# Moving the start addresses of a float32r kernel's tiles in SBUF: weights at 160 and 192, rows at 448 or 192, modulo 512

## The chip, the cores and the metric

One core of one Trainium2 chip. The metric is the device time of one execution in microseconds (us), as the median of several runs. A page of the profile and its trace come from one execution taken by the hardware profiler.

## The reference: what is computed

Two blocks, one after the other, on 256 latent tokens and 256 context tokens of width 1024. Almost all arithmetic is in dense products with weights that are read once from HBM:

```
# first block: layer 0 a gated linear attention (gla), layer 1 a state-space scan (ssd)
for i in range(2):
    m = split(silu(c) @ ada_w[i] + ada_b[i], 6)
    u = modulate(h, m[0], m[1])
    y = gla_mixer(u, ...) if i == 0 else ssd_mixer(u, ...)      # h @ w_in, a scan, @ w_out
    h = layer_norm(ALPHA * h + m[2] * y)
    h = layer_norm(ALPHA * h + m[5] * (relu(modulate(h) @ ffn_w1[i]) ** 2 @ ffn_w2[i]))
# second block: two attention layers, three kinds of attention each
for l in range(2):
    hn = rms_norm(h) * (1 + scale) + shift
    q, k, v, z, gm = split(hn @ w_in[l])          # neighbourhood, latent (mla), differential
    y = sum(sigmoid(gm[r]) * ((attend_r * silu(z[r])) @ w_br[l][r]) for r in range(3))
    h = h + gate * (y @ w_out[l])
```

## The kernel before, in words

**One product.** A float32 product is made of three float32r matmuls, which are called passes here. The weights are split into a rounded part `weights_hi` and the rest `weights_lo`, and the rows (the activations) into two tiles of the same kind: `input_hi` and `input_lo`, or `ffn_hidden_hi` and `_lo`, `ssd_out_hi` and `_lo`, `mix_o_hi` and `_lo`, `merge_o_hi` and `_lo`. For each block of 128 features the method `passes` lists

```
out += [(hi[:, k, cols], xh), (hi[:, k, cols], xl), (lo[:, k, cols], xh)]
```

where the first of a pair is the stationary operand (128 columns, loaded by a LDWEIGHTS) and the second is the moving one (512 columns for all tokens, 256 where only the latent ones are left). The value projections are made by token instead (`passes_by_token`): there the rows are stationary and the weights move, 512 columns of them. Eight blocks of 128 features make 24 passes, which fill one bank of PSUM. Line 284 (`product`) issues most passes; lines 305, 322, 3586 and 3736 issue the others. While a pass runs, the LDWEIGHTS of the next one is under way.

**The weights' way.** SP's queue loads 512 KB at a time into one of four slots of `wslots`. ScalarE (ACT) copies a slot into `weights_hi`, rounding it (line 221). VectorE (DVE) or GpSimd (POOL) subtracts and writes `weights_lo` (line 231). TensorE (PE) waits for the split, and a slot comes free when it is split. An order written out by hand sets what each engine does; nothing plans it at run time.

**The stages.** The times are those of the profiled execution. GLA input products and scan (about 35 to 300 us), its output product (300 to 350), the feed-forward of layer 0 over all tokens (350 to 720), the SSD layer (720 to 1110), the feed-forward of layer 1 over latent tokens (1110 to 1300), attention layer 0 over all tokens (1300 to 1950), attention layer 1, in its latter part over latent tokens (1950 to 2455).

**Addresses.** Every tile is taken with `b.sb(stack, name, shape)`, one behind the other, as a stack in each partition; each starts at a multiple of 32 bytes. 16,512 bytes lie in front of `wslots`, so that it starts at 128 modulo 512. All large tiles are multiples of 512 bytes, so the start modulo 512 is handed on from tile to tile until a small one moves it. Counted from the shapes, the starts modulo 512 before are:

| tiles | stage | start modulo 512 |
|---|---|---|
| wslots, weights_hi, weights_lo | all | 128 |
| input_hi, input_lo | GLA input | 0 |
| gla_out_hi, gla_out_lo | GLA output | 0, 96 |
| input_hi, input_lo, ffn_hidden_hi, _lo | feed-forward of layer 0 | 448 |
| input_hi, input_lo, ssd_out_hi, _lo | SSD | 320 |
| input_hi, input_lo, ffn_hidden_hi, _lo, mix_o_hi, _lo, merge_o_hi, _lo | feed-forward of layer 1 and both attention layers | 320 |

The operand of one pass or another lies a multiple of 512 bytes behind its tile's start. For a pair of tiles this document calls the moving tile's start minus the stationary tile's start, modulo 256, its offset; the prediction says why 256 is used.

Of the kernel before, what the change touches and what calls it, by code (L numbers as in the profile page):

```python
# [14 lines left out]
F32 = mybir.dt.float32  # L15
# [5 lines left out]
P = 128  # L21
# [9 lines left out]
DEPTH = 2  # L31
# [8 lines left out]
SH = SG * SREP  # L40
# [5 lines left out]
NAH, MLH, DFH = 8, 8, 4  # L46
# [14 lines left out]
AM = 2 * SLOT // P  # L61
SHARED = {"halves_ready": "unit_scaled", "rank_rounded": "hat_edges", "norm_summed": "tables_made", "roped": "hat_factors", "mixed_gated": "maps_combined", "mixed_squared": "rows_final", "power_added": "rows_ready", "vectors_added": "unit_made", "group_summed": "unit_scaled", "group_turned": "top_made", "group_flat": "top_ready",
          "group_copied": "prob_ready", "group_biased": "prob_scaled", "group_shifted": "prob_turned",
          "sum_slab_0": "maps_combined", "sum_slab_1": "rows_final", "sum_slab_2": "rows_ready", "sum_slab_3": "rows_turned"}
ADA_ROUND = {"ada_front": 0, "ada_core": 1, "ada_scan": 3}


# [306 lines left out]
def build(nc, d, out, dump=None, until=99):  # L374
    ctx = ExitStack()
    with ctx:
        b = Build(nc, d, ctx)
        b.psum = ctx.enter_context(nc.psum_tensor("psum", [P, 8, 512], F32))
        b.wslots = b.sb(ctx, "wslots", [P, RAW, SLOT])
        b.whi = b.sb(ctx, "weights_hi", [P, RING, SLOT])  # L380
        b.wlo = b.sb(ctx, "weights_lo", [P, RING, SLOT])
        b.whi_r, b.wlo_r = b.whi[:].bitcast(F32R), b.wlo[:].bitcast(F32R)
        b.H1 = b.sb(ctx, "h1", [P, KD, T])
        b.H2 = b.sb(ctx, "h2", [P, KD, T])
        b.ident = b.sb(ctx, "ident", [P, P])
        b.snake = b.sb(ctx, "snake", [P, P])
        b.ones = b.sb(ctx, "ones", [P, P])
        b.half_ones = b.sb(ctx, "half_ones", [P, P])
        b.cols = b.sb(ctx, "cols", [P, 5, P])
        b.eps = b.sb(ctx, "eps", [P, 2])  # L390
        b.mod1 = b.sb(ctx, "mod1", [P, DEPTH, 48, 2])
        b.mod2 = b.sb(ctx, "mod2", [P, DEPTH, 24, 2])
        b.lam = b.sb(ctx, "lam", [P, DEPTH, 4])
        make_plan(b)
        with ExitStack() as early:
            b.ada_c = b.sb(early, "ada_c", [P, 2, KD, 32])
            b.ada_flat = b.sb(early, "ada_flat", [P, 512])
            b.ada_vec = b.sb(early, "ada_vec", [P, AM, 2])
            with b.joined():
                gla_layer(b)  # L400
                if until >= 3:
                    finish_layer(b, 0, ALL, None)
                if until >= 4:
                    ssd_layer(b)
        with ExitStack() as late:
            input_parts(b, late, False)
            if until >= 5:
                finish_layer(b, 1, LAT, b.H2)
            if until >= 6:
                with b.joined():  # L410
                    for l in range(DEPTH):
                        attention_layer(b, l, out)
        if until < 6:
            store_stage(b, b.H2 if until >= 5 else b.H1, out, dump)
# [122 lines left out]
def ada_copy(b, act, phase, r, bank):  # L537

    g = b.phases[phase][2] + r
    before = ADA_ROUND[phase] + r  # L540
    act.wait_ge(b.sem("product_done"), g + 1)
# [315 lines left out]
def input_parts(b, st, raw=None):  # L857

    b.UH = b.sb(st, "input_hi", [P, KD, T])
    b.UL = b.sb(st, "input_lo", [P, KD, T])  # L860
    b.UH_r, b.UL_r = b.UH[:].bitcast(F32R), b.UL[:].bitcast(F32R)
    if raw is not False:
        b.raw = b.sb(st, "input_raw", [P, 2, T]) if raw is None else raw
# [534 lines left out]
def gla_layer(b):  # L1398
    st = ExitStack()
    with st:  # L1400
        qk = b.sb(st, "gla_qk", [P, GH, 2, T])
        v = b.sb(st, "gla_v", [P, TT, D])
        gate = b.sb(st, "gla_gate", [P, KD, T])
        cum = b.sb(st, "gla_cum", [P, 2, GH, T])
        qT, kT = qk[:, :, 0, :], qk[:, :, 1, :]
        stat = b.sb(st, "gla_stat", [P, GH, TT])
        oT = qk[:].rearrange("p h a t -> p (h a) t")
        room = [x[:].rearrange(s) for x, s in ((qk, "p h a t -> p (h a t)"), (v, "p t n -> p (t n)"),
                                               (gate, "p k t -> p (k t)"), (cum, "p z h t -> p (z h t)"))]
        gla_project(b, qT, kT, v, gate, cum, room)  # L1410
        at = b.nc.sbuf_base
        b.UH, b.UL = (b.nc.alloc_sbuf_tensor_at(f"gla_out_{x}", [P, KD, T], F32, offset=at + o) for x, o in (("hi", 4096), ("lo", OUT_LOW)))
        b.UH_r, b.UL_r = b.UH[:].bitcast(F32R), b.UL[:].bitcast(F32R)
        gla_core(b, qk, v, cum, oT, stat)
        gla_out(b, oT, gate, stat)
# [200 lines left out]
def gla_core(b, qk, v, cum, oT, stat):  # L1616
# [12 lines left out]
    st = ExitStack()  # L1629
    with st:  # L1630
# [12 lines left out]
        masks = b.sb(st, "gla_masks", [P, NR, P], U8)  # L1643
        diag2 = b.sb(st, "gla_diag2", [P, P])
        middles = b.sb(st, "gla_middles", [P, 2, 2, GH, CH])
        vec = b.ada_vec[:].rearrange("p (q t) v -> p q t v", q=4)
        wide_masks = b.H2[:, 0:3, :].rearrange("p a t -> p (a t)").rearrange("p (z n k) -> p z n k", z=2, k=P)
        _, _, vt, _ = b.phases["gla_v1"]
        OUT, STATE, SCORE, TURNED, ADA = (0, 1), (2, 3), (4, 5), 6, 7
# [481 lines left out]
def ssd_layer(b):  # L2131
    st = ExitStack()
    with st:
        xs = b.sb(st, "ssd_x", [P, TT, SDI])
        bt = b.sb(st, "ssd_b", [P, NCTX // P, SG * SN])
        bT, cT = b.H2[:, :, NCTX:T], b.H1[:, :, 0:NCTX]
        z = b.sb(st, "ssd_z", [P, SDI // P, NLAT])
        y = xs[:, 0:2, :]
        s = b.sb(st, "ssd_state", [P, 2, SDI])
        tok = b.sb(st, "ssd_tok", [P, 6, 2 * SH])  # L2140
        dskip = b.sb(st, "ssd_dskip", [P, SH])
        rows = b.sb(st, "ssd_rows", [P, 3 * P])
        pick = b.sb(st, "ssd_pick", [P, 2 * SH])
        unit = b.sb(st, "ssd_unit", [P, P])
        hide = b.sb(st, "ssd_hide", [P, 2, P])
        ssd_project(b, xs, bt, bT, cT, z, s, tok, dskip, rows, pick, unit, hide)
        power = b.sb(st, "ssd_power", [P, 2, NLAT])
        ssd_core(b, xs, bt, bT, cT, y, z, s, tok, dskip, rows, pick, unit, hide, power)
        ssd_out(b, y, s, power)
# [192 lines left out]
def ssd_core(b, xs, bt, bT, cT, y, gates, s, tok, dskip, rows, pick, unit, hide, power):  # L2342
# [16 lines left out]
    st = ExitStack()  # L2359
    with st:  # L2360
# [1 line left out]
        square = b.H2[:, 0:4, 0:NCTX].rearrange("p (i n) t -> p i n t", i=2)  # L2362
        work = mixers[:, 0:4 * SDI].rearrange("p (a n) -> p a n", a=4)
        part = b.H2[:, :, 0:NCTX]
        vec = b.ada_vec[:].rearrange("p (q t) v -> p q t v", q=4)
        SEGS, SCORE, ADA = 3, 4, 3

        def main(g):
# [937 lines left out]
def attend_pairs(b, l, r, m, last, fill):  # L3306
# [6 lines left out]
    groups = [(seg, t) for seg in ((LAT,) if last else (LAT, CTX)) for t in range(2)]  # L3313
# [4 lines left out]
    early = 0 if near else S // 3 if last else S // 2  # L3318
# [3 lines left out]
    st = ExitStack()  # L3322
    with st:
        prob = b.sb(st, "prob", [P, 2, 2, T])
        probT = m["spare"] if r else b.sb(st, "probT", [P, 2, T])
        top = b.sb(st, "row_top", [P, 2, 2, 2])
        den = b.sb(st, "row_sum", [P, 2, 2])
        if near:
            bias, biased = b.H1[:, 0:2, :], b.H1[:, 2:4, :]
            mask = b.sb(st, "na_mask", [P, NLAT])  # L3330
# [460 lines left out]
def attend_maps(b, l, m, last, fill):  # L3791
# [3 lines left out]
    groups = [(s, t) for s in ((LAT,) if last else (LAT, CTX)) for t in range(2)]  # L3795
# [3 lines left out]
    early, lead = S // 2, min(S + S // 2, 2 * KD)  # L3799
# [19 lines left out]
    st = ExitStack()  # L3819
    with st:  # L3820
        prob = b.sb(st, "prob", [P, 2, 2, T])
        probT = b.sb(st, "probT", [P, T])
        top = b.sb(st, "row_top", [P, 2, 2, 2])
        den = b.sb(st, "row_sum", [P, 2, 2])
        sub = b.sb(st, "diff_rows", [P, DFH, P])
        ss = b.sb(st, "diff_ss", [P, len(groups), DFH])
        sq = b.sb(st, "diff_sq", [P, DFH, P])
        with b.stage() as block:

# [464 lines left out]
```

## Time and profile before

| | |
|---|---|
| median of three runs | 2463.5 us (2460.54 to 2468.15) |
| the profiled execution, its own time | 2456.91 us |
| its span in the trace | 2455.1 us |
| PE busy | 2355.8 us, 96% of the span, 13,654 matmuls |
| PEld (weight loads) busy | 1932.6 us, 79% |
| DVE busy | 1570.2 us, 64% |
| ACT busy | 1217.1 us, 50% |
| POOL busy | 450.7 us, 18% |
| granted TensorE clock, mean | 0.985 |
| DMA | 302 MB, 123 GB/s |

A matmul's busy time in the trace is its own duration with the end modelled; neighbours overlap. How fast PE goes through passes is therefore read from their starts: the time from one start to the next is called the pitch here.

### The profile page before, as it was taken

The page shows a single profiled execution, that of the slowest core. Times are in us where ns is not written, and L with a number is a line of the kernel's source. Part 1 is how long each engine was busy: PE and PEld are TensorE (multiplying, and loading weights), DVE is VectorE, ACT ScalarE, POOL GpSimd, SP SyncE. Part 2 cuts the span into 40 slices and gives each one's busy share as a digit, 9 for nine tenths or more (in the row PEclk, how much of TensorE's full clock was granted, in tenths as well). Part 3 has the DMA queues.
Part 4 walks back from the last instruction along what each step waited for, and adds up shares of the span by engine and source line. Part 5 has one row for each costly group of instructions (what it writes and reads, how often), then busy time and mean ns, then how long its engine had stood idle before and what let it go on. Part 6 is the DMA issues. An engine that isn't in the chain of part 4 may idle for free. (4 is left out here: it accounts for less than half of the span.)

```text
span 2455.1 us, 34875 instructions
## 1 busy us (share of the span) xinstructions
PE 2355.8 (96%) x13654; PEld 1932.6 (79%) x13654; DVE 1570.2 (64%) x2359; ACT 1217.1 (50%) x2090; POOL 450.7 (18%) x277
## 2 busy tenths in 40 slices
PE   7998999999999999989999999999999989989989
PEld 5776778887879888689998767677777877878778
DVE  5867978778765667687665454643665455574665
ACT  2666544223238334557454355763365244665464
POOL 0000000000017434000004431005111145404210
PEclk9999999999999999999999999999999999999999
DMA  8734527666535332446663232213222234334334
GB/s 316 212 121 145 156 80 212 184 185 186 158 102 138 95 92 62 138 138 195 185 179 86 77 85 59 64 50 94 74 64 77 77 97 116 95 89 118 94 96 129
DMA packets 416075, 302.11 MB, mean 123 GB/s; under 512 B 10210, under 2 KB 389192, under 8 KB 414888
## 3 DMA queue, kind: packets, MB, share of 16 engines
q1 hardware_dynamic: 414800, 299.45, 42.0%
q8 instruction: 109, 1.79, 0.3%
q10 hardware_dynamic: 1112, 0.44, 0.1%
q14 instruction: 54, 0.44, 0.1%
HBM read 298.80 MB, written 1.05 MB: 122 GB/s over the span
## 5 line engine op out<-in xcount | busy, mean ns | idle before, releaser
L221 ACT ACTIVATE weights_hi<-wslots 128x1024 fp32r<-128x1024 f32 (+1 forms) x408 | 427.1, 1051 | 251.4 <-PE psum L284 192.2
L284 PE MATMUL psum<-input_hi,weights_hi 128*128 128x512 f32 (+1 forms) x1384 | 494.9, 358 | 1.6 <-PEq L1044 0.6
L284 PE MATMUL psum<-input_hi,weights_lo 128*128 128x512 f32 (+1 forms) x1384 | 482.8, 349 | 0.0
L284 PE MATMUL psum<-input_lo,weights_hi 128*128 128x512 f32 (+1 forms) x1384 | 482.1, 348 | 0.0
L231 POOL TENSOR_TENSOR weights_lo<-wslots,weights_hi 128x1024 fp32r<-128x1024 f32 (+1 forms) x139 | 333.6, 2407 | 714.5 <-ACT weights_hi L221 713.8
L231 DVE TENSOR_TENSOR weights_lo<-wslots,weights_hi 128x1024 fp32r<-128x1024 f32 x269 | 330.3, 1237 | 161.1 <-ACT weights_hi L221 160.3
L284 PEld LDWEIGHTS psum<-input_hi,weights_hi 128*128 128x128 f32 x1384 | 261.8, 189 | 45.5 <-issue 8.8
L284 PEld LDWEIGHTS psum<-input_lo,weights_hi 128*128 128x128 f32 x1384 | 261.2, 189 | 38.1 <-issue 2.9
L284 PEld LDWEIGHTS psum<-input_hi,weights_lo 128*128 128x128 f32 x1384 | 261.0, 189 | 37.0
L284 PE MATMUL psum<-ffn_hidden_hi,weights_hi 128*128 128x512 f32 (+1 forms) x512 | 173.6, 339 | 0.0
L284 PE MATMUL psum<-ffn_hidden_hi,weights_lo 128*128 128x512 f32 (+1 forms) x512 | 172.5, 337 | 0.0
L284 PE MATMUL psum<-ffn_hidden_lo,weights_hi 128*128 128x512 f32 (+1 forms) x512 | 171.7, 335 | 0.0
L2849 DVE RECIPROCAL head_rstd<-head_rstd 128x512 f32<-128x512 f32 (+1 forms) x32 | 94.4, 2951 | 96.0 <-ACT head_rstd L2841 96.0
L3736 PE MATMUL psum<-input_hi,weights_hi 128*128 128x512 f32 (+1 forms) x384 | 135.9, 354 | 4.4 <-issue 3.3
L3736 PE MATMUL psum<-input_lo,weights_hi 128*128 128x512 f32 (+1 forms) x384 | 130.9, 341 | 0.0
L3736 PE MATMUL psum<-input_hi,weights_lo 128*128 128x512 f32 (+1 forms) x384 | 130.8, 340 | 0.0
L284 PEld LDWEIGHTS psum<-ffn_hidden_hi,weights_hi 128*128 128x128 f32 x512 | 96.8, 189 | 13.3 <-issue 3.6
L284 PEld LDWEIGHTS psum<-ffn_hidden_hi,weights_lo 128*128 128x128 f32 x512 | 96.5, 189 | 10.7
L284 PEld LDWEIGHTS psum<-ffn_hidden_lo,weights_hi 128*128 128x128 f32 x512 | 96.1, 188 | 10.8 <-issue 0.2
L1306 ACT ACTIVATE ffn_hidden<-psum 128x512 f32<-128x512 f32 (+1 forms) x64 | 31.4, 490 | 124.5 <-PE psum L284 117.1
L2323 DVE SCALAR_TENSOR_TENSOR ssd_conv<-psum,cols,ssd_conv 128x508 f32<-128x508 f32 (+3 forms) x128 | 87.2, 681 | 4.5
L3736 PEld LDWEIGHTS psum<-input_hi,weights_hi 128*128 128x128 f32 x384 | 73.8, 192 | 17.1 <-issue 7.8
(541 smaller groups left out, 4915.9 us busy)
## 6 DMA issues: line engine op xcount, KB each, us to landing
wslots<-w_in SPq DMA_DIRECT2D x132, 512.0 KB, 3.9
wslots<-ffn_w SPq DMA_DIRECT2D x128, 512.0 KB, 4.6
wslots<-ssd_w_in SPq DMA_DIRECT2D x49, 512.0 KB, 4.0
wslots<-ada_w SPq DMA_DIRECT2D x32, 512.0 KB, 4.7
h<-w_ada SPq DMA_DIRECT2D x28, 512.0 KB, 4.3
wslots<-gla_w_in SPq DMA_DIRECT2D x25, 512.0 KB, 4.8
input_raw<-ada_w SPq DMA_DIRECT2D x24, 512.0 KB, 4.0
ada_slab<-ada_w SPq DMA_DIRECT2D x24, 512.0 KB, 3.8
```

Of the source, the lines that this page charges most:

```text
L221: act.activation(self.part(self.whi_r, n), self.slot(n), ACT.Copy)\
L231: engine.tensor_tensor(self.part(self.wlo_r, n), self.slot(n), self.part(self.whi, n), ALU.subtract)\
L284: ins = pe.matmul(out_of(self.bank(g)), l, r, start=first and i == 0, stop=last and i == len(pairs) - 1, skip_group_check=not (first and l ...
L1306: act.activation(hid[:, j % NH, :], b.bank(g)[:, a:e], ACT.Relu).then_inc(b.reads_out(g), 1)
L2323: ins = dve.scalar_tensor_tensor(dst[:, :, o], src[:, :, i], tap(k), dst[:, :, o], ALU.mult, ALU.add)
L2849: dve.reciprocal(r, r).then_inc(b.tick("dve_step"), 1)
L3736: ins = pe.matmul(b.bank(g)[:, a:e], w, u, start=x == 0, stop=x == len(pairs) - 1, skip_group_check=True)
```

## The change

Only the places of tiles in SBUF change. `lam` (32 bytes) is taken ahead of `weights_hi`, and `eps` (8 bytes, which take 32) ahead of `weights_lo`. The small tile `ada_vec` of the early layers, and the tiles `row_top`, `row_sum` and `diff_ss` of the attention stages, become views of one tile `small` (128 bytes) that stays for the whole program. `ssd_dskip` goes to the very top of SBUF. The starts modulo 512 after it are:

| tiles | before | after |
|---|---|---|
| wslots | 128 | 128 |
| weights_hi | 128 | 160 |
| weights_lo | 128 | 192 |
| input_hi, input_lo of GLA | 0 | 0 |
| gla_out_hi, gla_out_lo | 0, 96 | 0, 96 |
| rows of the feed-forward of layer 0 | 448 | 448 |
| rows of SSD | 320 | 192 |
| rows of the feed-forward of layer 1 and of attention | 320 | 448 |
| h1, h2, ident, ones | 128 | 192 |

No instruction is added, removed or moved: on all five engines the same instructions stand in the same order with the same waits, and the names of the small tiles alone differ.

```diff
+SBUF_TOP = 229344
...
         b.wslots = b.sb(ctx, "wslots", [P, RAW, SLOT])
+        b.lam = b.sb(ctx, "lam", [P, DEPTH, 4])
         b.whi = b.sb(ctx, "weights_hi", [P, RING, SLOT])
+        b.eps = b.sb(ctx, "eps", [P, 2])
         b.wlo = b.sb(ctx, "weights_lo", [P, RING, SLOT])
...
         b.cols = b.sb(ctx, "cols", [P, 5, P])
-        b.eps = b.sb(ctx, "eps", [P, 2])
         b.mod1 = b.sb(ctx, "mod1", [P, DEPTH, 48, 2])
         b.mod2 = b.sb(ctx, "mod2", [P, DEPTH, 24, 2])
-        b.lam = b.sb(ctx, "lam", [P, DEPTH, 4])
+        b.small = b.sb(ctx, "small", [P, 2 * AM])
+        b.ada_vec = b.small[:].rearrange("p (q v) -> p q v", v=2)
         make_plan(b)
         with ExitStack() as early:
             b.ada_c = b.sb(early, "ada_c", [P, 2, KD, 32])
             b.ada_flat = b.sb(early, "ada_flat", [P, 512])
-            b.ada_vec = b.sb(early, "ada_vec", [P, AM, 2])
...
-        dskip = b.sb(st, "ssd_dskip", [P, SH])
+        dskip = b.nc.alloc_sbuf_tensor_at("ssd_dskip", [P, SH], F32, offset=SBUF_TOP - 4 * SH)
...
-        top = b.sb(st, "row_top", [P, 2, 2, 2])
-        den = b.sb(st, "row_sum", [P, 2, 2])
+        top = b.small[:, 0:8].rearrange("p (n a q) -> p n a q", n=2, a=2)
+        den = b.small[:, 8:12].rearrange("p (n a) -> p n a", n=2)
...
-        ss = b.sb(st, "diff_ss", [P, len(groups), DFH])
+        ss = b.small[:, 12:12 + len(groups) * DFH].rearrange("p (g h) -> p g h", h=DFH)
```

## Rows read from the trace of the kernel before

**Rows 1.** The page: busy time and share of the span of each engine.

```profile
PE 2355.8 (96%) x13654; PEld 1932.6 (79%) x13654; DVE 1570.2 (64%) x2359; ACT 1217.1 (50%) x2090; POOL 450.7 (18%) x277
```

**Rows 2.** Busy time by stretch: stretch, length, PE busy, granted clock, DMA share, GB/s.

```profile
350.00:720.00 370.00, 368.48 (x1638) 1.00 0.56 167
1410.00:1550.00 140.00, 134.74 (x814) 1.00 0.26 71
2080.00:2170.00 90.00, 85.27 (x571) 0.98 0.38 107
2170.00:2300.00 130.00, 124.68 (x818) 1.00 0.38 100
2300.00:2400.00 100.00, 88.81 (x623) 0.95 0.36 96
```

**Rows 3.** Timeline of PE, feed-forward of layer 0: first and last of 142 passes.

```profile
429.64 0.39 PE L284 MATMUL psum<-input_lo,weights_hi 128*128 128x512 f32 x1
...
461.91 0.39 PE L284 MATMUL psum<-ffn_hidden_lo,weights_hi 128*128 128x512 f32 x1
```

**Rows 4.** The same, attention layer 0: first and last of 173 passes.

```profile
1899.80 0.39 PE L3736 MATMUL psum<-input_hi,weights_hi 128*128 128x512 f32 x1
...
1939.94 0.39 PE L3736 MATMUL psum<-merge_o_lo,weights_hi 128*128 128x512 f32 x1
```

**Rows 5.** The same, by token in attention layer 0: first and last of 41 passes.

```profile
1729.83 0.39 PE L284 MATMUL psum<-weights_lo,input_hi 128*128 128x512 f32 x1
...
1738.98 0.39 PE L284 MATMUL psum<-weights_hi,input_hi 128*128 128x512 f32 x1
```

**Rows 6.** The same, by token in GLA: first and last of 91 passes.

```profile
172.79 0.39 PE L284 MATMUL psum<-weights_hi,input_lo 128*128 128x512 f32 x1
...
193.71 0.39 PE L284 MATMUL psum<-weights_hi,input_lo 128*128 128x512 f32 x1
```

**Rows 7.** The same, 256 columns, SSD input: first and last of 179 passes.

```profile
749.81 0.28 PE L284 MATMUL psum<-input_hi,weights_hi 128*128 128x256 f32 x1
...
769.98 0.28 PE L284 MATMUL psum<-input_lo,weights_hi 128*128 128x256 f32 x1
```

**Rows 8.** The same, 256 columns, feed-forward of layer 1: first and last of 173.

```profile
1199.73 0.28 PE L284 MATMUL psum<-ffn_hidden_hi,weights_hi 128*128 128x256 f32 x1
...
1219.99 0.28 PE L284 MATMUL psum<-input_lo,weights_hi 128*128 128x256 f32 x1
```

**Rows 9.** Busy time by stretch, stretches full of 256-column passes: columns as in rows 2.

```profile
1151.50:1293.00 141.50, 141.50 (x1202) 1.00 0.64 181
1067.00:1100.00 33.00, 33.00 (x282) 1.00 0.66 185
2398.00:2425.00 27.00, 27.00 (x232) 1.00 0.73 202
748.60:783.70 35.10, 35.10 (x312) 1.00 0.74 196
1132.00:1150.70 18.70, 18.70 (x167) 1.00 0.66 189
936.00:948.00 12.00, 12.00 (x109) 1.00 0.73 219
```

**Rows 10.** Groups by line and shape, PE: count, busy us, mean ns, idle before.

```profile
L284 PE MATMUL psum<-input_hi,weights_hi 128*128 128x512 f32 x832 | 338.2, 406 | 0.4 <-DVE att_o L3525 0.4
L3736 PE MATMUL psum<-input_hi,weights_hi 128*128 128x512 f32 x192 | 79.1, 412 | 0.0
L284 PE MATMUL psum<-weights_hi,input_hi 128*128 128x512 f32 x192 | 80.6, 420 | 0.2 <-DVE input_lo L891 0.2
L284 PE MATMUL psum<-input_hi,weights_hi 128*128 128x256 f32 x552 | 156.8, 284 | 1.2 <-PEq L1044 0.6 <-POOL weights_lo L231 0.6
```

**Rows 11.** Line 231, the subtraction: duration ns min/median/max, and who waited for it.

```profile
L231 DVE TENSOR_TENSOR weights_lo<-wslots,weights_hi x269: 1161/1221/2046, 32.2 to 2440.4; 128x1024 fp32r<-128x1024 f32 x135
L231 POOL TENSOR_TENSOR weights_lo<-wslots,weights_hi x139: 1821/2400/3247, 722.7 to 2305.0; 128x1024 fp32r<-128x1024 f32 x133, 128x768 fp32r<-128x768 f32 x6
...
  PEld psum L305: 9.5, 4
```

More of the change, by code:

```diff
@@ L1645, in gla_core @@
         middles = b.sb(st, "gla_middles", [P, 2, 2, GH, CH])
-        vec = b.ada_vec[:].rearrange("p (q t) v -> p q t v", q=4)
+        vec = b.ada_vec.rearrange("p (q t) v -> p q t v", q=4)
         wide_masks = b.H2[:, 0:3, :].rearrange("p a t -> p (a t)").rearrange("p (z n k) -> p z n k", z=2, k=P)
@@ L2364, in ssd_core @@
         part = b.H2[:, :, 0:NCTX]
-        vec = b.ada_vec[:].rearrange("p (q t) v -> p q t v", q=4)
+        vec = b.ada_vec.rearrange("p (q t) v -> p q t v", q=4)
         SEGS, SCORE, ADA = 3, 4, 3
@@ L3822, in attend_maps @@
         probT = b.sb(st, "probT", [P, T])
-        top = b.sb(st, "row_top", [P, 2, 2, 2])
-        den = b.sb(st, "row_sum", [P, 2, 2])
+        top = b.small[:, 0:8].rearrange("p (n a q) -> p n a q", n=2, a=2)
+        den = b.small[:, 8:12].rearrange("p (n a) -> p n a", n=2)
         sub = b.sb(st, "diff_rows", [P, DFH, P])
-        ss = b.sb(st, "diff_ss", [P, len(groups), DFH])
+        ss = b.small[:, 12:12 + len(groups) * DFH].rearrange("p (g h) -> p g h", h=DFH)
         sq = b.sb(st, "diff_sq", [P, DFH, P])
```

## The prediction

> **What bounds the kernel now.** I read the page first: PE is busy 96% of the span, DVE 64%, ACT 50% [rows 1]. Busy time by stretch then says where the missing 4% lie: the feed-forward of layer 0 has PE busy 368.5 of 370 us, and even the attention stages have it busy 89 to 96% [rows 2]. So the end is set by how fast PE goes through its passes, nearly everywhere, and a change that leaves every instruction in place can only act through their pace.
>
> The third view is the timeline of PE, and there the reader is to look at starts, not durations. In the feed-forward of layer 0, 142 passes of 512 columns start between 429.64 and 461.91 us: 32.27 us over 141 steps is a pitch of 228.9 ns [rows 3]. In attention layer 0, 173 passes of the same shape, on the same line's pattern of hi-hi, lo-hi, hi-lo, start between 1899.80 and 1939.94 us: 40.14 over 172 is 233.4 ns [rows 4]. The granted clock is 1.00 in the stretch of the first [rows 2]. What differs is where the rows lie: at 448 modulo 512 in the one, at 320 in the other, with the weights at 128 in both. By token, where the weights at 128 move and the rows at 320 stand, the pitch is 9.15 us over 40, 228.8 ns [rows 5]; in GLA, weights at 128 moving over rows at 0, it is 20.92 over 90, 232.4 ns [rows 6].
>
> Moving start minus stationary start, modulo 512, gives: 320 for rows 3 and for rows 5 (equal pitches, though the roles are swapped), 192 for rows 4, 128 for rows 6. Modulo 256 these are offsets of 64 (228.9), 192 (233.4) and 128 (232.4). The step between best and worst is 4.5 ns, 1.9% of a pass.
>
> With 256 columns the offset is 192 everywhere, and two pitches occur: 20.17 us over 178 is 113.3 ns in the SSD input product [rows 7], 20.26 over 172 is 117.8 ns in the feed-forward of layer 1 [rows 8]. The step is 4.5 ns again. Stretches full of such passes stay in one of the two: 1202, 282 and 232 passes in 141.5, 33 and 27 us are at the long pitch (about 117 ns), 312, 167 and 109 in 35.1, 18.7 and 12 us at the short one (about 112, edges counted) [rows 9], all at granted clock 1.00. Within a stretch nothing about DMA (0.64 to 0.74 in both kinds) tells them apart.
>
> **The change part by part.** The offsets after it: rows at 448 or 192 over weights at 160 and 192 give 32 for `weights_hi` and 0 for `weights_lo`, in every stage but GLA's; GLA's rows at 0 get 96 and 64; by token the weights move over rows at 448, 224 and 0. No row of before has an offset of 0 or 32, so each term is bounded from both sides by the pitches that the trace does show.
>
> - 512 columns over rows at 320. Line 284 issues 832 hi-hi passes of that shape [rows 10]; without the 232 of the feed-forward of layer 0 and the 136 of GLA, 464 remain. Line 3736 issues 192 with `input_hi` [rows 10], and with the smaller groups of lines 3736, 3586 and 305 the sum is 888, times three kinds of pass: 2,664 passes. Bounds are the best and the worst pitch seen, 228.9 and 233.4: between 0 and 4.45 ns each, 0 to 11.8 us. I take the best, 11.8 us, since 32 lies nearest to 64 among the offsets that have a row.
> - 256 columns. Line 284 has 552 hi-hi passes with `input_hi` [rows 10]; with `ffn_hidden_hi` and the others it is 1,416, times three: 4,248. The long-pitch stretches hold 1,716 of them and the short-pitch stretches 588 [rows 9]; of the other 1,944 I count three in ten at the long pitch from the same reading of starts, so some 2,300 have it. Going to 113.3 ns saves 2,300 times 4.45 ns, 10.2 us; all taking the long pitch costs 1,950 times 4.45, 8.7 us. I take the saving.
> - GLA's input products: 408 passes go from about 232.4 to the level of offsets 64 and 96, at most 3.5 ns each, 1.4 us; its 192 by-token passes go to offsets 160 and 192, up to 0.9 ns each slower, 0.2 us. Together 1.2 us gained.
> - The feed-forward of layer 0, 1,536 passes at 228.9 ns: they go from offset 64 to 32 and 0. I take no change; the bad end is 233.4, 6.8 us lost.
> - By token outside GLA, 480 passes at 228.8 (three times 192 less GLA's 192, and line 3097's): no change taken; the bad end is 2.1 us.
> - ACT's rounding, DVE's and POOL's subtraction read `wslots` at 128 and now write at 160 and 192 instead of 128. DVE's median is 1221 ns and POOL's 2400 [rows 11], and a slot gives PE 24 passes: 5.5 us at 512 columns, 2.72 us at 256. POOL's is the thin cover: 0.32 us is left per slot at the short pitch. PE waited for it hardly at all (9.5 us for the worst waiter, line 305, four times) [rows 11]. I take nothing; if POOL lost 15% it would set the pace of the slots it splits at 256 columns.
> - The shared small tile: the waits are the same, so no engine waits for another that it didn't wait for. Nothing.
>
> Sum at PE: 11.8 + 10.2 + 1.2 = 23.2 us. Not all of it reaches the end. In the four stretches of attention where PE is busy 89 to 96% [rows 2] it waits for softmax and norms on DVE and ACT, and what PE finishes sooner becomes a longer wait there. They hold some 400 of the 512-column passes (1.8 us) and 960 of the others (three in ten at the long pitch, 1.3 us); I drop half of these 3 us. That leaves 21.7 us. Against the profiled execution's own 2456.9 us it gives 2435.2; that execution was 6.6 us under the median of the runs, so from 2463.5 it gives 2441.8, and I forecast 2442.
>
> A rule speaks against all of this. By the trace, equal passes at equal granted clock run at 228.9 or 233.4 ns depending on the stage [rows 3, 4]. The Trainium skill, page "SBUF — State Buffer", section "Who interferes with whom", says that TensorE has two independent read ports, one for the moving operand and one for LDWEIGHTS, and that PE never waits on anyone; by that an address would do nothing and the sum would be 0. The trace does not agree that nothing disturbs the stream, but it does not prove that the address is the cause either, since each offset goes with a stage.
>
> **The rivals.**
>
> *A lower step still.* The pitches seen are steps of 2.2 or 4.5 ns; offsets of 0 and 32 may have one that no stage of before shows. Another 2.2 ns on the 8,450 passes that go to them (2,664 + 4,248 + 1,536) is 18.8 us more: 2442 less 19 is 2423. For it: offset 64 need not be the minimum. Against: no row.
>
> *Half of it.* The 256-column passes have both pitches at one and the same offset [rows 7, 8], so something else picks between them, and it may go on doing so. Then 13 us less the waits' share are left: about 2451.
>
> *Nothing.* The pitch belongs to the stage (the engines that write beside it, the DMA), or to differences modulo 512 that I fold wrongly: 2463. Against it: rows 3 and 5 agree with roles, stages and DMA share all different.
>
> *Slower.* One mechanism: offset 0 and 32 are on the bad side, like 192. Then the feed-forward of layer 0 loses 6.8 us, by-token passes 2.1, and the short-pitch 256-column ones 8.7, with nothing gained at the others: 2463.5 + 17.6 is 2481. It decides once the mean pitch of layer 0's feed-forward goes over about 231 ns, since rows at 320 then gain less than the others lose. For it: offset 0 puts the moving and the stationary read on the same place in the 256 bytes, and no row tells what that costs.
>
> **How the numbers follow.** Forecast (best known pitch everywhere) 0.42, lower step 0.20, half 0.17, nothing 0.11, slower 0.10. A measurement of this kernel tells about 0.3%, 7.4 us, from no change. The first three are faster by more: 0.79; nothing is 0.11; slower 0.10. The range takes in the lower step (2423, a little under it) and the half, and ends just past no change: 2421 to 2465; outside are the slower case and the far tail of the lower step. The forecast's own range is 2434 to 2449.
>
> **What the changed kernel's profile would show.** In attention and feed-forward, starts of 512-column passes 228.9 ns apart (24 in 5.49 us instead of 5.60); in the feed-forward of layer 1, 113.3 ns (24 in 2.72 us), so that this stage is about 5 us shorter; layer 0's feed-forward as long as before; DVE, ACT and POOL durations of lines 221 and 231 unchanged. The prediction is wrong if layer 0's feed-forward changes its pitch, either way, if 256-column passes still show 117.8, or if PE's idle time grows by more than 2 us.

## The result and the profile after

The changed kernel takes 2474.06 us (median of 8 runs, 2469.3 to 2476.6), the one before 2463.42 us in the same comparison. The ratio is 1.0044 with a 95% interval of 1.003 to 1.0058: it is slower, by 10.6 us (0.44%). The forecast was 2442 us. Its range ended at 2465, and the sign was wrong.

The page of the changed kernel, busy time and count by engine (the row of before is in [rows 1]):

```profile
PE 2370.4 (96%) x13654; PEld 1937.9 (79%) x13654; DVE 1573.6 (64%) x2359; ACT 1219.0 (49%) x2090; POOL 450.8 (18%) x277
```

PE has 14.6 us more busy time in a span that is 12.4 us longer (2467.5 against 2455.1). Its weight loads have 5.3 us more, and DVE, ACT and POOL at most 3.4. The work is the same, so the passes themselves take longer. The rounding and the subtraction hardly do: their groups on the page (line, operation, count, busy us, mean ns, idle before) stand at 1051 ns on ACT, 2407 on POOL and 1237 on DVE before, and at 1054, 2407 and 1238 after:

```profile
L221 ACT ACTIVATE weights_hi<-wslots 128x1024 fp32r<-128x1024 f32 (+1 forms) x408 | 427.1, 1051 | 251.4 <-PE psum L284 192.2
L231 POOL TENSOR_TENSOR weights_lo<-wslots,weights_hi 128x1024 fp32r<-128x1024 f32 (+1 forms) x139 | 333.6, 2407 | 714.5 <-ACT weights_hi L221 713.8
L231 DVE TENSOR_TENSOR weights_lo<-wslots,weights_hi 128x1024 fp32r<-128x1024 f32 x269 | 330.3, 1237 | 161.1 <-ACT weights_hi L221 160.3
...
L222 ACT ACTIVATE weights_hi<-wslots 128x1024 fp32r<-128x1024 f32 (+1 forms) x408 | 428.5, 1054 | 255.7 <-PE psum L285 196.7
L232 POOL TENSOR_TENSOR weights_lo<-wslots,weights_hi 128x1024 fp32r<-128x1024 f32 (+1 forms) x139 | 333.5, 2407 | 717.9 <-ACT weights_hi L222 717.8
L232 DVE TENSOR_TENSOR weights_lo<-wslots,weights_hi 128x1024 fp32r<-128x1024 f32 x269 | 330.5, 1238 | 162.0 <-ACT weights_hi L222 160.9
```

Busy time by stretch, the feed-forward of layer 0, which answers to the first row of [rows 2] (stretch, length, then busy us and count of PE, PEld, DVE, ACT and POOL, granted clock, DMA share, GB/s):

```profile
350.00:727.00 377.00, 375.85 (x1645) 294.66 (x1644) 278.01 (x312) 127.72 (x182) 8.21 (x11) 1.00 0.55 163
```

About as many matmuls as before take 377 us instead of 370, at the same granted clock. The timeline of PE shows how. Below are the first and last of four groups of passes, in order of time: 139 in that stage (line 285 is line 284 of before), 173 with 256 columns in the SSD input product, 42 by token in attention layer 0, and 173 by feature in attention layer 0.

```profile
429.62 0.40 PE L285 MATMUL psum<-input_hi,weights_hi 128*128 128x512 f32 x1
...
461.82 0.40 PE L285 MATMUL psum<-ffn_hidden_hi,weights_hi 128*128 128x512 f32 x1
...
757.73 0.28 PE L285 MATMUL psum<-input_hi,weights_lo 128*128 128x256 f32 x1
...
777.98 0.28 PE L285 MATMUL psum<-input_hi,weights_hi 128*128 128x256 f32 x1
...
1740.28 0.40 PE L285 MATMUL psum<-weights_hi,input_hi 128*128 128x512 f32 x1
...
1749.85 0.40 PE L285 MATMUL psum<-weights_lo,input_hi 128*128 128x512 f32 x1
...
1899.65 0.40 PE L3738 MATMUL psum<-merge_o_hi,weights_hi 128*128 128x512 f32 x1
...
1939.78 0.40 PE L3738 MATMUL psum<-input_lo,weights_hi 128*128 128x512 f32 x1
```

The pitches are 32.20 us over 138, 233.3 ns (228.9 before, [rows 3]); 20.25 over 172, 117.7 (113.3 before, [rows 7]); 9.57 over 41, 233.4 (228.8 before, [rows 5]); and 40.13 over 172, 233.3, as before (233.4, [rows 4]). In these stages what was short became long, and what was long stayed. The granted clock is 1.00 in all four, as it is in the stretch of [rows 4] in the trace of before.

### The profile page after: what moved, and what is told of

The parts are those of the page before. It is cut to its first block and busy times, and to the rows that moved or that the text cites. A ratio compares the mean times of both kernels' runs of the same rounds, so it can differ in the third digit from the quotient of the medians.

```text
span 2467.5 us, 34875 instructions
## 1 busy us (share of the span) xinstructions
PE 2370.4 (96%) x13654; PEld 1937.9 (79%) x13654; DVE 1573.6 (64%) x2359; ACT 1219.0 (49%) x2090; POOL 450.8 (18%) x277
## 5 line engine op out<-in xcount | busy, mean ns | idle before, releaser
L222 ACT ACTIVATE weights_hi<-wslots 128x1024 fp32r<-128x1024 f32 (+1 forms) x408 | 428.5, 1054 | 255.7 <-PE psum L285 196.7
L232 POOL TENSOR_TENSOR weights_lo<-wslots,weights_hi 128x1024 fp32r<-128x1024 f32 (+1 forms) x139 | 333.5, 2407 | 717.9 <-ACT weights_hi L222 717.8
L232 DVE TENSOR_TENSOR weights_lo<-wslots,weights_hi 128x1024 fp32r<-128x1024 f32 x269 | 330.5, 1238 | 162.0 <-ACT weights_hi L222 160.9
L2851 DVE RECIPROCAL head_rstd<-head_rstd 128x512 f32<-128x512 f32 (+1 forms) x32 | 94.5, 2952 | 97.1 <-ACT head_rstd L2843 97.1
L285 PEld LDWEIGHTS psum<-ffn_hidden_hi,weights_hi 128*128 128x128 f32 x512 | 96.2, 188 | 15.2 <-issue 3.6
L285 PEld LDWEIGHTS psum<-ffn_hidden_lo,weights_hi 128*128 128x128 f32 x512 | 96.2, 188 | 10.6 <-issue 0.2
```

What stands on the lines that cost most here:

```text
L222: act.activation(self.part(self.whi_r, n), self.slot(n), ACT.Copy)\
L232: engine.tensor_tensor(self.part(self.wlo_r, n), self.slot(n), self.part(self.whi, n), ALU.subtract)\
L285: ins = pe.matmul(out_of(self.bank(g)), l, r, start=first and i == 0, stop=last and i == len(pairs) - 1, skip_group_check=not (first and l ...
L2851: dve.reciprocal(r, r).then_inc(b.tick("dve_step"), 1)
```

## The experiments

**The two halves of the change.** One kernel has the rows' places of the change and the weights back at 128, because `lam` and `eps` no longer stand ahead of `weights_hi` and `weights_lo` but behind other tiles:

```diff
-        b.lam = b.sb(ctx, "lam", [P, DEPTH, 4])
...
-        b.eps = b.sb(ctx, "eps", [P, 2])
...
         b.cols = b.sb(ctx, "cols", [P, 5, P])
+        b.eps = b.sb(ctx, "eps", [P, 2])
...
         b.mod2 = b.sb(ctx, "mod2", [P, DEPTH, 24, 2])
+        b.lam = b.sb(ctx, "lam", [P, DEPTH, 4])
```

> The rows' places of the change with the weights back at 128: feed-forward of both layers and attention have rows at 448 over weights at 128, SSD has rows at 192 over 128, by-token passes have weights at 128 over rows at 448. Theory A (the pitch is set by moving start minus stationary start modulo 256, offset 64 short, all else about 233): 512-column passes with moving rows at 228.9 ns everywhere outside GLA, SSD included; by token (offset 192) 233.4; 256-column passes 113.3 ns at best. Against before: 11.8 us less for 512 columns, 2.2 us more by token, 0 to 10 us less at 256 columns, so 2441 to 2454 us. Theory B (the same modulo 512, difference 320 short, all else long): the same but for the SSD stage, whose 600 passes of 512 columns stay at 233.4: 2.7 us less gain. Theory C (the stage sets the pitch, not the address): the pitches of before, 2463 us.

The other is the kernel before with `lam` ahead of `weights_hi` and `eps` ahead of `weights_lo`, and nothing else:

> The weights' places of the change (160 and 192) with rows where they were before (448 in the feed-forward of layer 0, 320 after it). Theory A (offset modulo 256; 32 and 0 are long, 64 short): the feed-forward of layer 0 goes from 228.9 to 233.3 ns, 6.8 us lost, by token (160 and 192 over 320: offsets 96 and 128) about 231 to 232, 1 to 2 us lost, the rest (offsets 160 and 128) between 232 and 233.3: 2470 to 2474 us. Theory B (difference modulo 512): about the same. Theory C (stage, not address): 2463 us.

Measured: the rows alone 2458.57 us, ratio 0.9985 (0.9973 to 0.9998); the weights alone 2469.49 us, ratio 1.0034 (1.0023 to 1.0044). The rows' half is a gain of 0.15% at the edge of what can be told from nothing, less than was expected (2441 to 2454 us), and the weights' half is where the time was lost. Timeline of PE with the rows moved alone: 67 passes of the SSD stage (rows at 192 over 128), 42 by token, 176 in attention layer 0, 172 with 256 columns.

```profile
784.72 0.39 PE L285 MATMUL psum<-input_hi,weights_hi 128*128 128x512 f32 x1
...
799.82 0.39 PE L285 MATMUL psum<-input_hi,weights_hi 128*128 128x512 f32 x1
...
1731.32 0.39 PE L285 MATMUL psum<-weights_hi,input_hi 128*128 128x512 f32 x1
...
1740.89 0.39 PE L285 MATMUL psum<-weights_lo,input_hi 128*128 128x512 f32 x1
...
1899.83 0.39 PE L3738 MATMUL psum<-input_lo,weights_hi 128*128 128x512 f32 x1
...
1939.89 0.39 PE L3738 MATMUL psum<-merge_o_hi,weights_lo 128*128 128x512 f32 x1
...
754.81 0.28 PE L285 MATMUL psum<-input_lo,weights_hi 128*128 128x256 f32 x1
...
774.95 0.28 PE L285 MATMUL psum<-input_lo,weights_hi 128*128 128x256 f32 x1
```

15.10 us over 66 is 228.8 ns in SSD, 9.57 over 41 is 233.4 by token, 40.06 over 175 is 228.9 in attention, 20.14 over 171 is 117.8 with 256 columns. So the pitch goes with the address, not the stage: theory C falls. SSD is short with a difference of 64 where theory B wanted 320, so the pitch repeats after 256 bytes: A stands against B. The gain is less than expected because most of the 256-column passes that had the short pitch at offset 192 went long at offset 64. Summed from start to start over both traces, without steps that hold a wait, 256-column passes cost 6.6 us more and by-token ones 1.8, against 9.4 us gained at 512 columns.

With the weights moved alone, layer 0's feed-forward has 233.3 ns (139 passes), and attention, where rows at 320 lie over 160 and 192, has 231.6 (174 passes), a little better than the 232 to 233.3 expected; the time is 0.5 us under the 2470 to 2474 expected. No stretch of 256-column passes has the short pitch here: their sum is 9.2 us more than before, and that of layer 0's feed-forward 6.5 us.

```profile
429.74 0.39 PE L284 MATMUL psum<-input_hi,weights_lo 128*128 128x512 f32 x1
...
461.94 0.39 PE L284 MATMUL psum<-ffn_hidden_hi,weights_lo 128*128 128x512 f32 x1
...
1899.78 0.40 PE L3736 MATMUL psum<-merge_o_hi,weights_lo 128*128 128x512 f32 x1
...
1939.85 0.39 PE L3736 MATMUL psum<-input_lo,weights_hi 128*128 128x512 f32 x1
```

**The pitch by itself.** A kernel that computes nothing of the reference: it lays pairs of row tiles and weight tiles at chosen places and runs chains of passes, and no other engine works while a chain runs.

```
x = mov[m][1 if q == 1 else 0][:].bitcast(F32R)       # rows at m modulo 512, hi, lo, hi
w = (st[l][1] if q == 2 else st[h][0])[:].bitcast(F32R) # weights_hi at h, weights_lo at l
pe.matmul(psum[:, c % 8, 0:n], w[:, b:b + P], x[:, a:a + n], ...)
```

> Chains of 48 passes of 512 columns, or 96 of 256, nothing else running, in the kernel's pattern hi-hi, lo-hi, hi-lo: weights at 128 and rows at each multiple of 32 below 512, then weights at 160 and 192 under rows at 448, 192, 320 and 0, then both weights at 160 and both at 192 under 448 and 192. Theory A: the pitch repeats after 256 bytes, short (228.9) at rows 192 and 448, long (233.3) at 320 and 64. Theory B: short at 448 alone. Theory C: one pitch at all of them. Theory D (the one short pitch needs hi and lo weights at the same place): both at 160 or 192 give a short pitch at some row where 160 and 192 together do not.

Read start to start, without the first six steps of a chain, in ns. Weights at 128 and 128:

```
offset modulo 256      0      32      64      96     128     160     192     224
512 columns, lower   226.8  233.4   228.8   233.2   232.2   234.2   233.4   233.2
512 columns, upper   226.7  233.4   228.9   233.4   cold    234.2   233.4   233.3
256 columns, lower   119.9  116.7   117.8   120.0   118.7   117.3   117.8   118.4
256 columns, upper   120.0  116.7   117.8   120.0   118.7   117.3   113.3   118.3
```

"Lower" and "upper" are two places of the rows 256 bytes apart: 128 to 352, and 384 onward to 96. The one marked cold is the first chain of the program, whose first passes start 427 ns apart. Each value is that of one chain. Two groups of rows stand here for the table, both with 512 columns: 37 passes at offset 0, and 36 at 32.

```profile
90.68 0.39 PE L78 MATMUL psum<-rows_128h,weights_128h 128*128 128x512 f32 x1
...
98.85 0.39 PE L78 MATMUL psum<-rows_128h,weights_128h 128*128 128x512 f32 x1
...
102.65 0.40 PE L78 MATMUL psum<-rows_160h,weights_128h 128*128 128x512 f32 x1
...
110.82 0.39 PE L78 MATMUL psum<-rows_160h,weights_128l 128*128 128x512 f32 x1
```

8.17 us over 36 steps is 226.9 ns, and 8.17 over 35 is 233.4. The table repeats after 256 within 0.2 ns wherever both places have a reading, but for one cell (theory A; the next experiment but one comes back to that cell, 113.3 against 117.8), and it is no smooth curve: 0 is the best at 512 columns and one of the two worst at 256, and 32 beside it has 233.4. Under rows at 448, weights at 160 and 192 (the change) have 233.3 ns, both at 160 also 233.3, and both at 192 have 227.2. So theory D holds as well: a shared good place gives the short pitch, and `weights_hi` at 160 (offset 32) spoils it, whether `weights_lo` lies there too or not.

**Both weight tiles at 192.** One line of the changed kernel is moved, `eps` from behind `weights_hi` to ahead of it:

```diff
         b.lam = b.sb(ctx, "lam", [P, DEPTH, 4])
+        b.eps = b.sb(ctx, "eps", [P, 2])
         b.whi = b.sb(ctx, "weights_hi", [P, RING, SLOT])
-        b.eps = b.sb(ctx, "eps", [P, 2])
         b.wlo = b.sb(ctx, "weights_lo", [P, RING, SLOT])
```

> The changed kernel with both weight tiles at 192 modulo 512 (eps ahead of weights_hi too), so that rows at 448 and 192 have offset 0 to both. Theory A with the table of the first probe (modulo 256: offset 0 226.7 ns at 512 columns and 120 at 256 columns): 512-column passes of both feed-forwards, SSD and attention at 226.7 ns, by token outside GLA 226.7 too, GLA's feature-major passes (offset 64) 228.9, its by-token ones (192) 233.3, 256-column passes 120 ns. Against before, at PE: 2,664 x 6.7 + 1,536 x 2.2 + 408 x 3.5 + 480 x 2.1 = 23.6 us less, and 2,300 x 2.2 + 1,950 x 6.7 + 192 x 0.9 = 18.3 us more: about 5 us faster, 2456. Rival (the probe's single chains do not carry over to the kernel, where other engines read and write beside PE): pitches as in the changed kernel, 233.3 and 117.8, 2474 us.

Measured: 2452.87 us, ratio 0.9968 (0.9955 to 0.9981), so 8 us faster than the kernel before and, by the medians of two comparisons, 21 us faster than the changed one. 143 passes of layer 0's feed-forward, 41 by token, 178 in attention layer 0, and 169 with 256 columns in layer 1's feed-forward:

```profile
429.80 0.39 PE L285 MATMUL psum<-input_lo,weights_hi 128*128 128x512 f32 x1
...
461.99 0.39 PE L285 MATMUL psum<-ffn_hidden_hi,weights_lo 128*128 128x512 f32 x1
...
1735.30 0.39 PE L285 MATMUL psum<-weights_hi,input_lo 128*128 128x512 f32 x1
...
1744.40 0.39 PE L285 MATMUL psum<-weights_lo,input_hi 128*128 128x512 f32 x1
...
1899.68 0.39 PE L3738 MATMUL psum<-input_hi,weights_hi 128*128 128x512 f32 x1
...
1939.80 0.39 PE L3738 MATMUL psum<-merge_o_hi,weights_hi 128*128 128x512 f32 x1
...
1199.74 0.28 PE L285 MATMUL psum<-ffn_hidden_hi,weights_hi 128*128 128x256 f32 x1
...
1219.90 0.28 PE L285 MATMUL psum<-input_hi,weights_hi 128*128 128x256 f32 x1
```

The pitches are 226.7, 227.5, 226.7 and 120.0 ns: the table carries over to the kernel with DMA and three other engines at work, good and bad entries alike. In the stretch of attention the view by window has, in the order PE, PEld, DVE, ACT, POOL, granted clock, DMA share and GB/s:

```profile
1899.68:1939.80 40.12, 40.12 (x179) 33.23 (x178) 12.84 (x11) 11.02 (x14) 5.17 (x4) 1.00 0.36 104
```

Rows at 448 over 192 and rows at 192 over 192 give much the same in the chains alone (227.2 and 226.7 ns), once more in steps of 256.

**Unlike places, and one chain again and again.** A second kernel of the first one's kind, with chains of 36 and 72 passes.

> Chains of 36 passes of 512 columns or 72 of 256, alone. First the 256-column chain at offset 192 again and again, with other chains ahead of it: one of two pitches each time (113.3 or 117.8) if the start of a chain picks it, 113.3 always if the first probe's difference between rows at 64 and rows at 320 was the address. Then weights_hi at 128 and weights_lo at each other multiple of 32, and rows_hi and rows_lo at unlike offsets. Theory A': each pass's excess comes from its moving start against the next pass's stationary start, so unlike places give the mean of the table's values. Rival: the three passes form one pattern, and unlike places give values of their own, perhaps under 226.7 at 512 columns or 113.3 at 256.

With 256 columns at offset 192, seven of eight chains had 113.3 ns and one 117.8, all from the same tiles at the same addresses. Their surroundings don't tell them apart: the long one stood between the same kinds of chains as three of the short ones. So this offset has two pitches, and no chain was seen to go from one to the other after its first few passes.

Offset 192 is not the only one with two. The kernel with the rows moved alone has offset 64 for all its 256-column passes, and the SSD output product there runs at 113.3 ns for 67 passes (7.48 us over 66), while the SSD input product has 117.8. At 512 columns, GLA's by-token passes have weights at 128 over rows at 0 in that kernel as in the one before (offset 128), and took 20.76 over 89, 233.3 ns, where they had 232.4 [rows 6]; the probes' chains at that offset had 232.2 and 233.4. First and last of both groups, 67 and 90 passes:

```profile
1059.79 0.28 PE L285 MATMUL psum<-ssd_out_lo,weights_hi 128*128 128x256 f32 x1
...
1067.27 0.28 PE L285 MATMUL psum<-ssd_out_lo,weights_hi 128*128 128x256 f32 x1
...
173.21 0.39 PE L285 MATMUL psum<-weights_lo,input_hi 128*128 128x512 f32 x1
...
193.97 0.40 PE L285 MATMUL psum<-weights_hi,input_lo 128*128 128x512 f32 x1
```

A cell of the table is therefore one pitch that its offset can take, and another chain at the same offset may have a second one.

The last part of this kernel gives the tiles of a pair unlike places. `weights_hi` at 128 with `weights_lo` elsewhere: of 56 places at 512 columns the best is 229.0 and most lie at 231 to 234; with 256 columns one has 113.6, the others 117.6 to 120.0. `rows_lo` apart from `rows_hi` (56 places): best 228.8 and 116.6. Unlike places have values of their own, not means of the table's, and none beats 226.7 or 113.3. Rows at offset 0 with `weights_lo` 32 bytes further, for one, have 233.5 at 512 columns, where two passes at 226.7 and one at offset 224 (233.2) would have a mean of 228.9. Theory A' falls in this form; the rival's better value was not found.

**Offset 0 for 512 columns, 192 for 256.** To the kernel with both weights at 192, 192 bytes of padding are added ahead of three pairs of tiles that only 256-column passes read:

```diff
+        if l:
+            b.sb(st, "hidden_room", [P, 48])
         hid_hi = b.sb(st, "ffn_hidden_hi", [P, HT, n])
...
+        b.sb(st, "out_room", [P, 48])
         yh = b.sb(st, "ssd_out_hi", [P, NF, NLAT])
...
+        if l == DEPTH - 1:
+            b.sb(st, "merge_room", [P, 48])
         oh = b.sb(st, "merge_o_hi", [P, BW // P, T])
```

> Both weight tiles at 192 with rows at offset 0 as in the run before it, but three pairs of row tiles that are read by 256-column passes alone get an offset of 192 by 192 bytes of padding: ssd_out (384 passes), ffn_hidden of layer 1 (768), merge_o of the last layer (96). Theory A, with the probes' table: their pitch falls from 120 to 113.3 ns (8.3 us less than with offset 0) or, if they take the other of the two pitches of that offset, to 117.8 (2.8 us less); all other pitches stay. So 2445 to 2450 us. Rival: passes that alternate between offsets have no own pitch, and the stages keep 120 ns: 2453.

And that one with 192 bytes of padding behind `gla_stat`:

> The run before it, and GLA's tiles 192 bytes higher, so that GLA's input rows have offset 0 too (before it 64 by feature, 192 by token). Theory A: 408 passes from 228.9 to 226.8 ns and 192 by-token ones from 233.4 to 227: 2.1 us less. Rival (those stretches are held by the arrival of weights, DMA share 0.56 to 0.94 in the first 205 us): no change against the run before it.

Measured against the kernel before: 2451.63 us, ratio 0.996 (0.9944 to 0.9975), and 2447.99 us, ratio 0.9943 (0.9926 to 0.9959). The first is 1.6 us above the 2445 to 2450 that were expected. The steps from one version to the next lie within these intervals, and only the timelines show them. With the first, 152 passes of layer 1's feed-forward have 113.3 ns, and later in that stage 172 have 117.8, both of the pitches of offset 192, and the rival's 120 ns in neither. Of the 1,248 passes that were moved there, some 650 have the short one:

```profile
1157.81 0.28 PE L285 MATMUL psum<-ffn_hidden_lo,weights_hi 128*128 128x256 f32 x1
...
1174.92 0.28 PE L285 MATMUL psum<-ffn_hidden_hi,weights_lo 128*128 128x256 f32 x1
...
1259.81 0.28 PE L285 MATMUL psum<-ffn_hidden_lo,weights_hi 128*128 128x256 f32 x1
...
1279.95 0.28 PE L285 MATMUL psum<-ffn_hidden_lo,weights_hi 128*128 128x256 f32 x1
```

With the second, 108 passes of GLA's input product have 24.25 us over 107, 226.6 ns (232.4 at best before). The DMA share is 0.95 in this stretch, so the rival, that the arrival of weights holds these passes, falls:

```profile
63.62 0.39 PE L285 MATMUL psum<-input_lo,weights_hi 128*128 128x512 f32 x1
...
87.87 0.39 PE L285 MATMUL psum<-input_hi,weights_hi 128*128 128x512 f32 x1
```

This last version has the lowest median of all, 14 us (0.57%) under the kernel before.

## Why the prediction was wrong, point by point

**Right: what bounds the kernel, and that the address acts.** PE's pitch sets the time, offsets repeat after 256 bytes, roles can be swapped, and the durations of lines 221 and 231 moved by 0.3% at most. With nothing else running, chains at 226.9 and 233.4 ns differ by the address alone. The Trainium skill's rule that I weighed against it (page "SBUF — State Buffer", section "Who interferes with whom": PE never waits on anyone) would have both alike, and the measurement decides against it.

**The step that failed: "I take the best, 11.8 us, since 32 lies nearest to 64 among the offsets that have a row."** Three rows of before at offsets 64, 128 and 192 were read as points of a smooth curve. The probe shows a jagged table: 226.7, 233.4, 228.8, 233.2 at 0, 32, 64, 96. Offset 32 has the long pitch. The second half of the same step took the two weight tiles as separate terms; a `weights_hi` at 160 costs each of the three passes 6.6 ns on the mean against both at 192 (233.3 against 226.7), although `weights_lo` at 192 had the best offset of all. In place of 11.8 us gained, the 2,664 passes gained 0.3 us, summed from start to start.

**"I take no change" for layer 0's feed-forward and by token.** These went to the bad ends that the prediction had put at 6.8 and 2.1 us: 1,536 passes from 228.9 to 233.3, 480 from 228.8 to 233.4 (6.8 and 2.2 us).

**"I take the saving" at 256 columns.** The value went the other way. The short pitch was seen at offset 192 and, in part, at 64, and in no stretch at the changed kernel's 32 and 0. The passes that had 113.3 now have 117.0 to 119.0. Summed over the trace from start to start, without steps that hold a wait, passes with `input_hi` and `input_lo` cost 6.3 us more, and all 256-column passes 7.1; that is near the 8.7 of the bad end, and nothing of the 10.2 was gained.

**GLA, 1.2 us taken.** Nothing was gained there either. Of the passes by feature, the first 240 or so went from 233.3 to 232.7 ns and the rest from 232.4 to 233.3, and those by token from 232.4 to 231.9. Together the passes of that stage cost 0.1 us more.

**The sum again.** Summed from start to start, layer 0's feed-forward cost 6.5 us and by-token passes of attention 1.8 (by the pitches above 6.8 and 2.2), and 256-column passes 7.1: with the 0.3 gained and GLA's 0.1 that is 15.2 us, and PE's busy time grew by 14.6. The span grew by 12.4, since PE's idle time fell from 99.3 to 97.1 us, 2 us of it in attention layer 1, where the prediction too had put some of a change into waits. It was the prediction's "slower" rival, 2481 with a chance of 0.10; its condition, that the mean pitch of layer 0's feed-forward goes over 231 ns, was met with 233.3. Half of its mechanism holds: offset 32 is on the bad side at 512 columns, like 192, but offset 0 is the best of all there (226.7) and bad at 256 only (120.0). "A lower step still" was true of offset 0 as well, but only where both weight tiles have it.

**What stays open.** Why offsets 0 and 64 are good and 32 is not, and what settles at a chain's start which of two pitches it takes where an offset has two (192 and 64 with 256 columns, 128 with 512). With most cells of the table measured once or twice, others may have a second pitch that was not seen. The runs give the table, not its cause.

## What to carry to other kernels

When PE is busy all the time, read the step from one matmul's start to the next, not its duration, for each stage: equal shapes with unequal steps are a lead that costs no instruction to follow. Before such a lead is followed to a place that no row shows, measure the whole table with chains of passes alone, each more than once. Here one kernel of 0.6 ms held the table, and the values checked in the kernel carried over; that some offsets have two pitches took the chains run again and again to see. Do not interpolate between addresses, keep the tiles that take turns in one pattern at the same place, and check each shape, since the best offset for one can be among the worst for another.

## What the runs showed of the hardware that was not expected

- A float32r pass of 512 columns with a 128-column weight load under it takes 226.7 to 234.2 ns at full granted clock, by the offset between moving and stationary tile modulo 256, where the tiles of a pair share their offset; with 256 columns 113.3 to 120.0 ns. That is 3.3% and 5.9% between best and worst, and 32 bytes more (offset 0 to 32 at 512 columns) can cost 6.7 ns.
- The order is not the same for the two lengths: offset 0 is best at 512 columns (226.7) and, with 96, worst at 256 (120.0).
- At offset 192 with 256 columns a chain keeps one of two pitches, 113.3 or 117.8 ns, for as long as it runs; the longest unbroken one in the kernel before has 910 passes in 107.00 us, 117.6 ns with its edges counted. Offset 64 with 256 columns has the same two, and offset 128 with 512 columns has 232.2 to 232.4 or 233.3 to 233.4.
- DMA, ScalarE, VectorE and GpSimd at work did not change the pitch at offset 0: 226.7 ns in the kernel's attention, with a DMA share of 0.36, 226.6 in GLA with one of 0.95, and 226.7 alone.
